# Low parts of every second u tile ahead of time, and the gate matrix stored from GpSimd's queue

## The reference

```python
qb = (xb @ w_q).reshape(TOKEN_BLOCK, PEER_HEADS, 2, PEER_DKEY)
s = jnp.einsum('thcd,hcnd->thcn', qb, sub_keys)
s_top, i_top = lax.top_k(s, PEER_TOPK)
cand = s_top[:, :, 0, :, None] + s_top[:, :, 1, None, :]
best, pos = lax.top_k(cand.reshape(...), PEER_TOPK)
eidx = jnp.take_along_axis(cand_idx, pos, axis=-1)
g = jax.nn.softmax(best, axis=-1)
h = gelu(einsum('td,thkd->thk', xb, u[eidx]))
return einsum('thk,thkd->td', g * h, v[eidx])
```

## Time and profile before

| | |
|---|---|
| median of 3 runs | 1596.01 us (1592.0 to 1598.8) |
| profiled execution, its time | 1596.0 us |
| its span in the trace | 1594.2 us |
| PE busy | 1572.1 us, 99% |
| DVE busy | 1319.1 us, 83% |
| ACT busy | 647.3 us, 41% |
| POOL busy | 486.9 us, 31% |
| moved by DMA | 452.24 MB, mean 284 GB/s |

### The profile page before, as it was taken

How to read it: one execution, slowest core, us unless ns; L and a number is a source line. 1 busy time by engine, 2 the same in 40 slices (tenths; PEclk the granted TensorE clock), 3 DMA queues, 4 the chain that set the end, 5 groups by cost and what they waited for, 6 DMA issues and landing times.

```text
span 1594.2 us, 24556 instructions
## 1 busy us (share of the span) xinstructions
PE 1572.1 (99%) x9566; PEld 1394.9 (88%) x9566; DVE 1319.1 (83%) x2408; ACT 647.3 (41%) x1012; POOL 486.9 (31%) x243
## 2 busy tenths in 40 slices
PE   9999999999999999899999999999999999999998
PEld 8897977888989999899999999999988888888886
DVE  6564366345899999999998889999999999999997
ACT  5634355532223343345555334333333343343332
POOL 4433223352235038511010333333332332232200
PEclk9999999999999999999999999999999999999999
DMA  7872212145132998699998999999999999999971
GB/s 280 298 276 79 77 54 80 60 153 185 54 93 77 318 312 276 255 325 318 352 351 268 350 421 423 407 408 405 406 420 409 396 397 414 395 390 416 400 296 54
DMA packets 148547, 452.24 MB, mean 284 GB/s; under 512 B 12112, under 2 KB 73808, under 8 KB 127184
## 3 DMA queue, kind: packets, MB, share of 16 engines
q1 hardware_dynamic: 120528, 282.86, 49.0%
q0 software_dynamic: 23296, 151.04, 23.6%
q10 hardware_dynamic: 4608, 16.78, 2.6%
HBM read 395.55 MB, written 54.53 MB: 282 GB/s over the span
## 4 chain that ended last, share of the span: by engine, by line
PE 77%; DVE 18%; DMA 3%; issue 1%; ACT 1%; POOL 0%; SPq 0%; DVEq 0%; POOLq 0%; ACTq 0%
PE bank L1518 23%; PE bank L1520 23%; PE bank L1519 23%; PE bank L1824 3%; DMA h_scratch<-hout 2%; DVE idx L1259 1%; DVE idx L1251 1%; DVE val L1250 1%; DVE val L1258 1%; DVE tmp L1252 1%; DVE uvb L1363 1%; DVE wlo L1345 1%; PE bank L1660 1%; PE bank L1647 1%; PE bank L1617 1%
## 5 line engine op out<-in xcount | busy, mean ns | idle before, releaser
L1518 PE MATMUL bank<-xhi,whi 128*128 128x352 f32 (+1 forms) x1408 | 489.7, 348 | 9.8 <-DVE wlo L1345 5.9
L1520 PE MATMUL bank<-xhi,wlo 128*128 128x352 f32 (+1 forms) x1408 | 481.9, 342 | 0.0
L1519 PE MATMUL bank<-xlo,whi 128*128 128x352 f32 (+1 forms) x1408 | 481.7, 342 | 0.0
L760 POOL DMA_INDIRECT uvb<-in_uv,eidx x128 | 214.6, 1677 | 551.6 <-DVE acc L1391 405.7
L970 ACT ACTIVATE whi<-raw 128x1024 fp32r<-128x1024 f32 x220 | 231.8, 1056 | 179.5 <-PE bank L1520 156.2
L1518 PE MATMUL bank<-whi,ahi 128*128 128x512 f32 x762 | 296.6, 389 | 0.0
L1519 PE MATMUL bank<-wlo,ahi 128*128 128x512 f32 x762 | 296.5, 389 | 0.0
L1520 PE MATMUL bank<-whi,alo 128*128 128x512 f32 x762 | 296.5, 389 | 0.0
L1518 PEld LDWEIGHTS bank<-xhi,whi 128*128 128x128 f32 x1408 | 266.3, 189 | 26.8 <-DVE wlo L1345 6.2
L1519 PEld LDWEIGHTS bank<-xlo,whi 128*128 128x128 f32 x1408 | 266.8, 189 | 14.9
L1520 PEld LDWEIGHTS bank<-xhi,wlo 128*128 128x128 f32 x1408 | 266.1, 189 | 15.4
(11 more groups left out here) (229 smaller groups left out, 2007.3 us busy)
## 6 DMA issues: line engine op xcount, KB each, us to landing
raw<-in_u SPq DMA_DIRECT2D x118, 512.0 KB, 6.8
raw<-in_uv SPq DMA_DIRECT2D x102, 512.0 KB, 9.7
g_scratch<-stage SPq DMA_DIRECT2D x48, 512.0 KB, 6.8
gl<-g_scratch SPq DMA_DIRECT2D x32, 768.0 KB, 8.6
raw<-in_w_in SPq DMA_DIRECT2D x22, 1024.0 KB, 5.4
h_scratch<-hout SPq DMA_DIRECT2D x96, 192.0 KB, 6.1
hl<-h_scratch SPq DMA_DIRECT2D x24, 768.0 KB, 10.8
x<-in_uv SPq DMA_DIRECT2D x25, 512.0 KB
```

What stands on the lines that cost most here:

```text
L760: nc.gpsimd.indirect_dma_start(out=uvb[:, r % UVB, :], out_offset=None, in_=a["uv"][:, :], in_offset=bass.IndirectOffsetOnAxis(ap=eidx[:, ...
L1518: mm(out, lh, rh, start=first, stop=False)
L1519: mm(out, lh, rl, start=False, stop=False)
L1520: return mm(out, ll, rh, start=False, stop=last)
```

## The change

Three things change, with the amount of work the same. First, the 16 tiles whose low parts are made during the projections are no longer 6 to 21 but 6, 8, 10 and so on to 36 (`PRE`). GpSimd makes those between (`POOL_LOWS`: 0 to 5, then 7, 9 and so on to 37). Second, the 48 stores of the gate matrix are issued from GpSimd's queue and no longer from SP's, and the gathers are written out by step (`gather_step`), with the stores between them. Third, a few steps move: the exponential from step 36 to 37, and the dot products of the last 32 tokens from steps 37, 38, 39, 40, 41, 43 to 38, 39, 40, 41, 42, 43.

```diff
-PRE_FIRST, PRE_END = 6, 22
-NPRE = PRE_END - PRE_FIRST
+PRE = list(range(6, 37, 2))
+NPRE = len(PRE)
+POOL_LOWS = [n for n in range(DVE_LOW) if n not in PRE]
+C_IDX_TILE, C_LOADS = 17, (25, 27, 31, 33, 37)
-EXP_STEP = 36
+EXP_STEP = 37
-C_STEPS = [37, 38, 39, 40, 41, 43] + [46 + 3 * i for i in range(NCP - 6)]
+C_STEPS = [38, 39, 40, 41, 42, 43] + [46 + 3 * i for i in range(NCP - 6)]
+def sets_in(step):
+    for k in range(SETS):
+        last = next(t for t in range(NT) if QS * (k + 1) - 1 in quads_after(t))
+        if step == last + 1:
+            yield k
+def gather_step(r):
+    if r < UVB + NCP:
+        return C_STEPS[r - UVB] - 3
+    return SUM_STEPS[(r - UVB - NCP) // 2] - 2
...
-                if PRE_FIRST <= s < PRE_END:
-                    sp.wait_ge(h_done, s - 3)
-                    sp.dma_start(tile_bufs(s)[2].bitcast(F32), lo_dram[s - PRE_FIRST]).then_inc(lo_in[s % 4], 16)
+            def low_load(s):
+                sp.wait_ge(h_done, s - 3)
+                sp.dma_start(tile_bufs(s)[2].bitcast(F32), lo_dram[PRE.index(s)]).then_inc(lo_in[s % 4], 16)
...
                 if s + 4 < RING5:
                     tile_load(s + 4)
+                if s + 3 in PRE:
+                    low_load(s + 3)
...
-                for k, i in set_of_step(s):
-                    g_store(k, i)
...
+            def g_store(k, i):
+                pool.wait_ge(g_free, QS * (k + 1))
+                nc.gpsimd.dma_start(g_dram[quads, :, k, :, :].rearrange("q m n t -> m q n t"),
+                             stage[:, k % 2, rows, :].rearrange("m (q n) t -> m q n t", n=4)).then_inc(g_stored[k % 2], 16)
+            for s in POOL_LOWS:
+                tile_low(s)
+                if s == C_IDX_TILE:
+                    pool.wait_ge(cidx_done, 1)
...
+                if s in C_LOADS:
+                    gather_u(C_LOADS.index(s))
+            for s in range(2 * NT):
+                while r < NCP + NG and gather_step(r) <= s:
...
+                for k in sets_in(s):
+                    for i in range(4):
+                        g_store(k, i)
```

More of the change, by code:

```diff
@@ L469, in wait_low @@
         def wait_low(engine, s):
[L471 to L474, removed]
+            if s in PRE:
+                engine.wait_ge(lo_in[s % 4], 16 * len([t for t in PRE if t <= s and t % 4 == s % 4]))
             elif s < DVE_LOW:
-                engine.wait_ge(low_pool, s + 1 - NPRE)
+                engine.wait_ge(low_pool, POOL_LOWS.index(s) + 1)
             else:
@@ L603, in tile_load @@
                     wait_low(sp, s - 5)
-                elif PRE_FIRST <= s - 4 < PRE_END:
+                elif s - 4 in PRE:
                     sp.wait_ge(tile_hi, s - 3)
@@ L622, in h_store @@
                 sp.dma_start(h_dram[n // 4][:, n % 4, :], hout[:, n % 4, :]).then_inc(h_stored[n % 4], 16)
[L624 to L630, removed]
             def h_load(m):
@@ L644, in g_load @@
                 sp.dma_start(gl[:, i % 2, :, :, :], g_dram[v_tile(4 * i) // 4]).then_inc(g_in[i % 2], 16)
[L646 to L652, removed]
             sp.wait_ge(ln_out, TC)
@@ L762, in gather @@
                     in_offset=bass.IndirectOffsetOnAxis(ap=eidx[:, k:k + 1], axis=0)).then_inc(uv_in[r % UVB], 16)
-            for s in range(PRE_FIRST):
-                tile_low(s)
[L766 to L780, removed]
-                    for g in range(CG):
-                        nc.gpsimd.dma_start(ch[CP:P, g * CT:(g + 1) * CT], cgel[g * CT:(g + 1) * CT, :]).then_inc(ch_in, 16)
+            def g_store(k, i):
+                pool.wait_ge(g_free, QS * (k + 1))
+                rows = slice(i * (NT // 4), (i + 1) * (NT // 4))
+                quads = slice(i * (NT // 16), (i + 1) * (NT // 16))
+                nc.gpsimd.dma_start(g_dram[quads, :, k, :, :].rearrange("q m n t -> m q n t"),
+                             stage[:, k % 2, rows, :].rearrange("m (q n) t -> m q n t", n=4)).then_inc(g_stored[k % 2], 16)
@@ new lines, in _ @@
+            for s in POOL_LOWS:
+                tile_low(s)
+                if s == C_IDX_TILE:
+                    pool.wait_ge(cidx_done, 1)
+                    for g in range(CG):
+                        nc.gpsimd.dma_start(cidx4[g * CT:(g + 1) * CT, :], cidx[CP:P, g * CT:(g + 1) * CT]).then_inc(cidx_in, 16)
+                    pool.wait_ge(cidx_in, 16 * CG)
+                if s in C_LOADS:
+                    gather_u(C_LOADS.index(s))
+            r = UVB
+            for s in range(2 * NT):
+                while r < NCP + NG and gather_step(r) <= s:
+                    if r < NCP:
+                        gather_u(r)
+                    else:
+                        if r == NCP:
+                            pool.wait_ge(idx_done, 1)
+                        gather(r - NCP)
+                    if r - NCP == UVB - 1:
+                        pool.wait_ge(cdot_gelu, 1)
+                        for g in range(CG):
+                            nc.gpsimd.dma_start(ch[CP:P, g * CT:(g + 1) * CT], cgel[g * CT:(g + 1) * CT, :]).then_inc(ch_in, 16)
+                    r += 1
+                for k in sets_in(s):
+                    for i in range(4):
+                        g_store(k, i)
@@ L842, in pre_load @@
                     act.wait_ge(pre_out[i % 6], 16 * (i // 6))
-                act.dma_start(pre_raw[:, i % 6, :], a["u"][PRE_FIRST + i]).then_inc(pre_in[i % 6], 16)
+                act.dma_start(pre_raw[:, i % 6, :], a["u"][PRE[i]]).then_inc(pre_in[i % 6], 16)
             def pre_store(i):
```

## The result

| | before | after |
|---|---|---|
| median | 1592.52 us (1589.45 to 1600.68, 20 runs) | 1598.68 us (1595.09 to 1601.72, 20 runs) |
| ratio | | 1.0031, 95% interval 1.0021 to 1.0040 |
| profiled execution | 1596.0 us | 1599.0 us, span 1597.2 |

The change makes the kernel slower by 0.3%, where 1587.6 us and a gain were forecast. The time itself lies in the range. By the prediction's bound of 0.5% it is no difference, but the interval excludes 1.

What follows compares the result with a forecast made beforehand. PE was taken as the bound, short of work only at 624 to 696 and 896.7 to 944.2 among places the change touches. From the profiled 1596.0 us, 1596.0 - 5.9 - 2.5 = 1587.6 us, range 1583 to 1600.

Steps and rivals of the forecast that it cites:

- first term: Selections and weights, 624 to 696: fewer DVE waits on GpSimd let the third batch of one-hots end earlier, -5.9 us.
- 15 x 0.8 = 12 us: In the selections: 15 lone GpSimd low parts cost DVE 0.8 us of waiting each, 12 us where there were 23.8.
- case 3: Port waits stay at 1.5 us each, selections end at 650, first term only -2: 1591.5 us, chance 0.14.
- The exponential as the limit: Before the weights: ACT's exponential is done at 653.6, so any end of the selections before 646.7 is good enough.
- second term: 896.7 to 944.2: stores off SP's queue recover half of PE's 5.3 us lost, -2.5 us, bounds 0 and -5.3, or +4.
- case 5: Gathers behind the last set's stores come late and DVE stops PE, +4: 1594 us and a little more, chance 0.02.
- DVE runs some three tiles ahead of PE: 896.7 to 944.2: DVE's lead of about 11 us can absorb some delay of gathers behind the last set's stores.
- third sign of being wrong: The prediction is wrong if DVE waits for gathers between 900 and 930 long enough to stop PE.
- Case 2: Selections gain, but full DMA and the gathers give back what SP wins after 896.7: 1590.1 us, chance 0.25.
- What a store costs GpSimd: Issuing one gate store takes GpSimd 1.9 us, bounds 0.5 and 7.4; four per set fit and cost nothing.
- case 4: Issuing a store takes GpSimd more than about 3.5 us, so ACT stops at `stage`, and PE: 1631 us, chance 0.12.
- Nothing else moves PE: SP's loads of ready low parts, GpSimd's lone low parts and the indices all come in time, costing PE nothing.

Runs made afterwards that it cites:

- e6: The kernel before, unchanged, profiled a second time: profiled execution 1586.9 us, fourth selection ended at 643.2.
- e7: e3b with GpSimd's low parts from tile 7 on cut to 8 of 1024 columns, the rest left out: median 1590.7 us, ratio to before 0.9986.
- e3b: The changed kernel with the gate stores of the last set alone back on SP's queue: median 1592.9 us, ratio to before 1.0008.
- e14: e12 with the exponential at step 35 instead of 36: median 1584.3 us, ratio to before 0.9967.
- e1: The changed kernel with all gate stores back on SP's queue, the alternating low parts kept: median 1595.3 us, ratio to before 1.0016.
- e2: The changed kernel with low-part tiles, indices and first gathers as before, so essentially only the stores moved: median 1601.7 us, ratio to before 1.0059.
- e15: e12 with the gate stores of all twelve sets on SP's queue: median 1585.6 us, ratio to before 0.9974.
- e12: The changed kernel with last-set stores on SP, `hout` store before tile load from step 80, GpSimd low parts in four pieces, exponential at step 36: 1585.8 us, ratio 0.9947.
- e10: The kernel before with each GpSimd low part from tile 22 on made by four instructions of 256 columns: median 1594.4 us, ratio to before 1.0016.
- e8: The changed kernel with the last set's four gate stores on GpSimd two steps later, behind two further gathers: median 1596.1 us, ratio to before 1.0011.

## Why the prediction was wrong

Counted from the profile of before, 1596.0 - 3.6 + 6.6 = 1599.0 us, the profile of after. Of the 11.4 us to the forecast of 1587.6 the first term makes 2.3 and the second 9.1.

- **The base.** The sum starts at "the profiled execution's 1596.0 us", "which equals the median": that was the median of 3 runs, and with 20 it is 1592.5. The profile was a slow draw; four of the 20 took longer. The first term priced what the change removes by this one draw, the 44.6 us selection of the earlier trace rows. Against the quick one (e6) the change loses 5.8 us at the fourth selection. This doesn't move the forecast time, but it is why even the part of the gain that came true is no gain over the median.
- **"15 x 0.8 = 12 us" of waits.** Mis-sized: 20.9 us, 1.4 each, at the bound of "15 x 1.5 = 22 (650)", and `eidx` is at 649.0. The 0.8 came from seven low parts as they happened to fall, and two of them (the x2 at 580.75 in the earlier trace rows) weren't alone. Even spacing does not make the meetings random: the waits themselves stretch a selection to four periods. So of the first term of -5.9 there came 652.3 - 649.0 = 3.3 in the selections and 3.6 at tile 85, against that profile; this was case 3's mechanism. Against a median run, for which 1592.5 - 421.1 - 278.2 = 893.2 is an estimate of tile 85, it is nothing (893.2 in after).
- **The exponential as the limit.** "done at 653.6" was right (653.03 + 0.63), and "646.7 is good enough" is borne out by e7, where DVE waits for it. Since the selections ended later, it wasn't reached in after.
- **The second term, -2.5: the step that failed most.** Wrong sign: +6.6 in the stretch. SP was freed as forecast: its issues are 0.33 us, and the 7.8 us wait of gelu at 917.5 is gone. But that wait didn't matter much: e3b still has one of 6.1 us there, and one of the two shortest stretches. The true price was case 5, "the gathers behind the last set stop DVE", which had a chance of 0.02 and a bound of +4. The step that failed is "DVE runs some three tiles ahead of PE, about 11 us, and can give up some of it". It counted the issues ahead of the gather, four of 1.9 us (measured 3.6 us together), and not the landing of 2 MB ahead of it in the same queue, which made 16.8 us of 10. The third sign of being wrong, a wait of DVE for gathers between 900 and 930, came true (5.8 us, ended at 918.15). What follows DVE's stop was also not worked out: SP's loads, and the stores behind them. PE stopped for a gelu and not for DVE.
- **Case 2, DMA full.** Not what happened: e14 comes to tile 85 11.4 us before the profile of before, and its stretch is 279.0, 0.8 longer.
- **What a store costs GpSimd, 1.9 us.** It is 0.90, so case 4 is out by far, and with it the thought that each of the 1024 runs has its price. The page's packet counts fit this: in after the queue that GpSimd issues to has 6912 packets more for 25.2 MB, 3.6 KB each, while packets under 2 KB fell from 73808 to 24656. The rule of the Trainium skill (SBUF — State Buffer, section "SBUF: two separate sides"), by which GpSimd can't write descriptors while DVE is in a two-port mode, had led to the higher of two values. 48 issues took 885 to 982 ns beside the one-hots, and no wait shows; whether DVE was ever in such a mode beside them no run shows, so the rule itself isn't tested. The lock on the port pair, from the same section, agrees with the rows: e7 takes nearly all of the subtractions away and 20.9 us of waits with them.
- **"Nothing else moves PE"** held: the indices, the loads of low parts and `stage` cost nothing that shows (ACT waited once, 1.6 us).

From the median of before, low parts about 0 and stores +6.6 give 1599.1, and 1598.7 was measured; but the "about 0" is itself worked out from that median, so the sum is no check of its own. The halves run alone don't add up: e1 (low parts) and e2 (stores) took 3.7 and 10.2 us more than before in their batch, the whole change 6.2 in its own. By e1's ratio the new low parts even cost a little. Why e2 is so slow, with tile 85 at 896.1 and its six runs within 2.2 us, is open. Open too is why e1's tile 85 comes 1.5 us after e3b's when only eleven sets differ in their queue; in e15 tile 85 comes no later than in e12 (887.0 and 887.8).

## What to carry to other kernels

Before pricing what a change removes, see whether the profile is a typical execution: compare its time with many runs, and profile twice. Where one engine's rhythm meets another's, the sum of waits can be a draw, and a number from one trace is one draw of it. A large transfer put ahead of another in a queue can cost that one in landing, and not in issue; look for who waits for it, and try the last transfers in a queue where nobody does. A repair at one place pays only up to the next limit: here four pieces on alternate tiles ended the selections 12.5 us sooner and tile 85 only 2.2, and one step of the exponential then won 4.6 us by medians.

## What was not expected of the hardware

A small DVE instruction can be passed over while GpSimd runs instruction after instruction: 0.28 us of work waited out twelve subtractions, 9.03 us in all (e10, 635.80). But it isn't always so. In the same execution `jf` was let in after one of twelve that followed each other (0.62 us, 598.28), and in before `picks` ended 0.15 us after the second of three, DVE first and then GpSimd:

```profile
616.32 4.80 DVE L1326 TENSOR_TENSOR picks<-sel,idf 128x128 f32<-128x128 f32 x1
616.19 7.20 POOL L738 TENSOR_TENSOR wlo<-raw,whi 128x1024 fp32r<-128x1024 f32 x3
```

What decides between the two no run shows. And the hold goes both ways: in e10 seven subtractions of 0.74 us took 7.9 us beside `ge`, `prod` and `picks` of DVE, each of which was delayed by at most 0.55 us in that stretch. A gather behind 2 MB of stores in its queue took 16.8 us to land, in after and in e8 alike, where gathers of before took 8.7 to 12.1.
